# Sample attention: the K and V page loads issued by one engine, GpSimd, with the next chunk's K ahead of the chunk's V

## What is computed

```python
def _sample_attend(q, k, v, lam, rel_bias, cache_k, cache_v, page_table):
    def one(args):
        pt, qi, ki, vi = args
        kp = cache_k[pt].reshape(past, N_ATT_HEADS, 2, ATT_HEAD_DIM)
        vp = cache_v[pt].reshape(past, N_ATT_HEADS, ATT_V_DIM)
        kf = jnp.concatenate([kp, ki.astype(kp.dtype)], axis=0)
        vf = jnp.concatenate([vp, vi.astype(vp.dtype)], axis=0)
        return _diff_attention(qi[None], kf[None], vf[None], q_pos, k_pos, rel_bias, lam)[0]
    return lax.map(one, (page_table, q, k, v))
```

## Time and profile before

| | |
|---|---|
| runs, median (lowest to highest) | 3984.93 us (3982.57 to 3989.07) |
| profiled execution, its own time | 3991.51 us |
| its span, first to last instruction | 3989.5 us |
| the stage `sample_attention` in it | 649.3 to 1019.6 us |
| busy over the span: PE, DVE, ACT, POOL | 60%, 64%, 37%, 33% |
| traffic of the core's DMA engines over the span | 337 GB/s |

### The profile page before, as it was taken

How to read it: one execution, slowest core, us unless ns; L and a number is a source line. 1 busy time by engine, 2 the same in 40 slices (tenths; PEclk the granted TensorE clock), 3 DMA queues, 4 the chain that set the end, 5 groups by cost and what they waited for, 6 DMA issues and landing times. The chain is left out here.

```text
span 3989.5 us, 55293 instructions
## 1 busy us (share of the span) xinstructions
PE 2409.4 (60%) x16678; PEld 1084.2 (27%) x16678; DVE 2542.6 (64%) x6416; ACT 1465.6 (37%) x4223; POOL 1296.8 (33%) x1334
## 2 busy tenths in 40 slices
PE   5999776898765354553564465465356456446543
PEld 3446445565322121220121121122112112112110
DVE  1111165666475888677677677767757767767775
ACT  0110053333003455543434444444444344444443
POOL 0000001444002344443444344444344444444442
PEclk7999978999887565775675676566567567657655
DMA  9102134999328899999999999999999999999998
GB/s 359 49 33 61 24 1 144 407 411 387 138 92 315 353 396 404 421 420 421 411 417 413 419 415 418 403 421 412 421 407 418 419 406 420 421 420 414 419 412 333
DMA packets 245932, 1343.89 MB, mean 337 GB/s; under 512 B 47288, under 2 KB 60825, under 8 KB 94084
## 3 DMA queue, kind: packets, MB, share of 16 engines
q0 software_dynamic: 164352, 1174.49, 71.4%
q1 hardware_dynamic: 64072, 147.14, 10.9%
q10 hardware_dynamic: 17212, 18.74, 1.4%
HBM read 1319.30 MB, written 20.97 MB: 336 GB/s over the span
## 5 line engine op out<-in xcount | busy, mean ns | idle before, releaser
L1595 PE MATMUL psum<-sb_ring,sb_fold_weighted 128*32 128x256 f32 x8448 | 1008.9, 569 | 1307.6 <-PEq L62 1203.0
L1563 POOL DMA_INDIRECT sb_ring<-in_uv,sb_experts x1056 | 1151.4, 1090 | 1655.6 <-POOLq L62 1504.6
L1780 DVE CUSTOM_DVE_ANT_0 sb_ring<-sb_ring,sb_h_four 128x1024 f32<-128x1024 f32 x1056 | 1265.8, 1225 | 652.6 <-DMA sb_ring<-in_uv,sb_experts 615.4
L1595 PEld LDWEIGHTS psum<-sb_ring,sb_fold_weighted 128*32 128x32 f32 x8448 | 268.6, 134 | 2012.8 <-issue 2003.2
L1685 ACT ACTIVATE sb_gelu<-sb_dots 128x1 f32<-128x1 f32 x1056 | 210.3, 199 | 994.4 <-ACTq L62 985.8
L806 POOL DMA_DIRECT2D sb_v_pages<-in_cache_v x256 | 135.0, 527 | 861.5 <-issue 683.5
L1690 ACT ACTIVATE sb_fold_weighted<-sb_fold,sb_expert_w 128x32 f32<-128x32 f32 x1056 | 339.3, 321 | 34.4
L1618 PE MATMUL psum<-sb_w_pq,sb_h2T 128*128 128x512 f32 x576 | 336.6, 738 | 1.5 <-issue 1.5
L1687 ACT ACTIVATE sb_expert_w<-sb_gelu,sb_gates 128x1 f32<-128x1 f32 x1056 | 311.1, 295 | 34.5
L1664 ACT COPY sb_h_four<-sb_h_tiles 32x1024 f32<-32x1024 f32 x180 | 187.5, 1042 | 4.2
L1618 PEld LDWEIGHTS psum<-sb_w_pq,sb_h2T 128*128 128x128 f32 x576 | 132.4, 242 | 193.4 <-issue 193.4
(11 more groups left out here) (227 smaller groups left out, 2646.7 us busy)
## 6 DMA issues: line engine op xcount, KB each, us to landing
sb_k_pages<-in_cache_k SPq DMA_DIRECT2D x256, 256.0 KB, 6.1
sb_v_pages<-in_cache_v POOLq DMA_DIRECT2D x256, 256.0 KB, 6.2
sb_w_ada<-in_w_ada SPq DMA_DIRECT2D x12, 2048.0 KB, 17.0
sb_ring<-in_uv,sb_experts POOLq DMA_INDIRECT x1056
sb_w_qkv<-in_w_in SPq DMA_DIRECT2D x3, 2048.0 KB, 19.3
sb_w_bcu<-in_w_in SPq DMA_DIRECT2D x12, 512.0 KB, 6.3
sb_w_pq<-in_w_pq SPq DMA_DIRECT2D x3, 2048.0 KB, 17.1
sb_h_tiles<-h_scratch SPq DMA_DIRECT2D x9, 512.0 KB, 9.2
```

The lines of the kernel that those rows point to most:

```text
L1563: pool.indirect_dma_start(ring[:, slot, :], None, uv, bass.IndirectOffsetOnAxis(ap=experts[:, u, g, n:n + 1], axis=0))\
L1595: ins = nc.tensor.matmul(psum[q * NS:(q + 1) * NS, bank, at:at + QUARTER], fw[:, slot, :], ring[:, slot, D + q * QUARTER:D + (q + 1) * QUA ...
L1780: dot = nc.vector.tensor_tensor_reduce(ring[:, slot, 0:D], ring[:, slot, 0:D], h2x[:, half], 1.0, 0.0, ALU.mult, ALU.add, dots[:, slot:slo ...
```

## The change

K's loads leave SP and go to POOL. POOL first runs the K load of chunk 0; then for each k it runs the K load of chunk k+1 and then the V load of chunk k. SP keeps the small tables, which it now fetches one after another. The helper `load`, the slots, the sizes and everything the other engines do are as they were.

```diff
@@ -814,19 +814,19 @@
                 sp.dma_start(rel[0:BUCKETS, :], A["rel_bias"]).then_inc(T["small"], 16)
                 sp.dma_start(hot[:], A["const_tail"]).then_inc(T["small"], 16)
                 sp.wait_ge(T["tab"], 16)
-                cache_k = A["cache_k"][0].rearrange("g p h m d -> g p (h m d)")
-                for k in range(STEPS):
-                    load(sp, cache_k, kp, k_land, k_free, k)
-                    if k == 0:
-                        sp.wait_ge(T["rows_zero"], 1)
-                        for h in range(H):
-                            sp.dma_start(rows[head(h, M), :], A["const_rows"][h * M:(h + 1) * M, :]).then_inc(T["small"], 16)
+                sp.wait_ge(T["rows_zero"], 1)
+                for h in range(H):
+                    sp.dma_start(rows[head(h, M), :], A["const_rows"][h * M:(h + 1) * M, :]).then_inc(T["small"], 16)
 
             @block.gpsimd
             def _(pool):
                 pool.wait_ge(T["tab"], 16)
                 cache_v = A["cache_v"][0].rearrange("g p h d -> g p (h d)")
+                cache_k = A["cache_k"][0].rearrange("g p h m d -> g p (h m d)")
+                load(pool, cache_k, kp, k_land, k_free, 0)
                 for k in range(STEPS):
+                    if k + 1 < STEPS:
+                        load(pool, cache_k, kp, k_land, k_free, k + 1)
                     load(pool, cache_v, vp, v_land, v_free, k)
```

## The result

| | before | changed |
|---|---|---|
| median of the runs | 3983.75 us (4 runs) | 4251.77 us (4 runs, 4246.65 to 4255.52) |
| profiled execution: time, span | 3991.51, 3989.5 us | 4251.70, 4249.7 us |
| `sample_attention`, its first DMA to the next stage's first | 371.4 us | 636.0 us |
| from there to the end | 2968.8 us | 2969.5 us |

The ratio is 1.067, with a 95% interval of 1.0651 to 1.0688. The loss lies in the one stage: 264.6 us. The stage itself began 5.1 us sooner in this execution (644.2 instead of 649.3 us), and what follows took 0.7 us more.

What follows compares the result with a forecast made beforehand. POOL's issue stream was to bound the stage: 127 loads at 4.51 us, plus a slower first pair and breaks, 592 us, ending the stage 251 us later; adjusted to the runs' median, 4236 us, range 4214 to 4285 us.

Steps and rivals of the forecast that it cites:

- The bound: In `sample_attention`, POOL's stream issues two loads per step, 9.02 us against 5.2 us now, and becomes the slowest part.
- the two limits: In the stage before the change, TensorE busy 251.35 of 280 us and DMA traffic at 410 GB/s, both near their limit.
- The price of a load: On POOL's sequencer, 4.51 us per load: four page numbers about 2.2 us, four DMA instructions 2.26 us.
- The breaks: In POOL's stream of 128 loads: 24 short ones of 0.3 us, 7 us, and four long ones, 12 us.
- The sum: POOL's first load to its 128th: 572.8 + 0.4 + 7 + 12 = 592 us, moving the stage's end by 251 us.
- POOL finds its slots free: In POOL's queue, V loads would not wait for slots, since 7.8 us a step is under 9.26.
- the loop through V's slots: From `values` through V's and K's loads, landing and TensorE's pass: 7.8 us a step, 8.5 with a lower clock.
- The clock: TensorE, idle part of each step, begins passes at 1.2 GHz; a pass lasts some 6.3 us, still hidden.
- rival 1: TensorE stays at the lower clock all pass, 10.1 us a step, so POOL waits for V slots: 4292 us; chance 0.11.
- Rival 2: In the stage, POOL isn't the bound and K waits may be saved: 3969 to 3985 us; chance 0.03.
- point of decision: On POOL's sequencer, 2.6 us per load, two in a 5.2 us step, from which the not-slower case decides.
- Rival 3: Page numbers hidden, but one queue ties K's lead to V's slots: 6.7 us a step, 4087 us; chance 0.03.

## Why the prediction held, and where it didn't

*The bound.* Right: POOL's issue stream became the bound. Of the two limits that I had named for the kernel before, the run with K's pages in plain order points to TensorE's pass and not to the data rate. 4236 us were predicted, 4252 measured; the stage was forecast 251 us longer and was 264.6 us longer.

*The price of a load.* Right: 4.51 us in the changed kernel as in the earlier trace rows, for K and V alike. The run with added reads shows that its idle half is the reads (2.18 us for four), and the version with fixed pages that it goes with them.

*The breaks.* Four long ones, as forecast, of 4.88 to 5.18 us: 2.6 us over the plain idle time of 2.25 in three of them and 2.9 in the fourth, 10.8 us in all and not 12. The count was a guess from two, and it held. The short ones stand again at the forecast rate, every 5.3 loads.

*The sum.* 592 us forecast from the first to the last load's DMA, 603.7 measured. What failed is the step "POOL finds its slots free". By the earlier trace rows I had put the loop through V's slots at 7.8 to 8.5 us a step, under 9.26. But TensorE's pass at the end of a sample is longer, and at the lower clock the loop goes over. At 742.30 it shows: the K load issued at 726.63 reached TensorE at 733.00, 6.4 us later (I had 5.8), and POOL's V load went out 9.3 us after that (I had 6.3 for the pass and 0.5 for the step to POOL):

```profile
726.63 2.26 POOL L806 DMA_DIRECT2D sb_k_pages<-in_cache_k  x4 [2.55 <-issue]
...
733.00 3.67 PE L849 MATMUL psum<-sb_ident,sb_k_pages 128*128 128x128 f32 x16 [5.41 <-DMA sb_k_pages<-in_cache_k]
...
740.57 1.06 PE L897 MATMUL psum<-sb_v_pages,sb_probsT 128*8 128x128 f32 x32
```

The 17 loads have 51.3 us of idle time, of which 17 x 2.25 = 38 are reads; 13 us are waiting, 10 of them at the ends of the first seven samples. Four V slots took just these 13 us away, and left 590.3 us from the first to the last load's DMA, against the 592 of the sum. The tail after the last load was 1.9 us longer, too (27.9 instead of 25.9 us, from the last load to the next stage), as TensorE came to it at the lower clock (its last `values` took 1.88 us instead of 1.06). 12 + 2 us are the difference in the stage.

*The clock.* Right in kind, and true of some passes only: many passes after idle time begin at the lower level (1.2 GHz). Here, in the changed kernel, 16 transposes after 5.08 us of idle time take 3.67 us; after 2.17 us they take 3.49:

```profile
903.73 3.67 PE L849 MATMUL psum<-sb_ident,sb_k_pages 128*128 128x128 f32 x16 [5.08 <-DMA sb_k_pages<-in_cache_k]
...
907.34 1.94 PE L859 MATMUL psum<-sb_k_pagesT,sb_q_rows 128*32 128x512 f32 x8
...
913.13 3.49 PE L849 MATMUL psum<-sb_ident,sb_k_pages 128*128 128x128 f32 x16 [2.17 <-DMA sb_k_pages<-in_cache_k]
...
916.55 1.06 PE L859 MATMUL psum<-sb_k_pagesT,sb_q_rows 128*32 128x512 f32 x8
```

The score behind them is once at 1.94 us and once at 1.06: some passes are slow in part only, as I took for all, and some further on, as rival 1 had for all. And some aren't slow at all: of the 61 whole groups of transposes from 660 us on 23 took 1.94 to 1.97 us, after up to 3.15 us of idle time, and 38 took 2.7 to 3.7; of the 64 scores 40 took 1.06 or 1.07. So the forecast's picture, every pass low at its start and high at its end, was a mean between the two kinds, and near enough.

*The rivals.* Rival 2's point of decision, 2.6 us for a load, agrees with the runs with four V slots: at 2.1 us a load the version is at the old time, at 3.4 us (reading once) it isn't. Its gain didn't come. Rival 3 had the mechanism right and the size wrong. Its 6.7 us a step were made of a landing of 3.5 us after the last DMA and of a pass at the upper clock, 4.84 us. Measured with fixed pages: V's DMAs 2.1, K's first DMA to TensorE 6.3, a pass at partly lower clock 6.2, the step to POOL 0.3, 14.9 us for two steps. It is mostly the pass that was mis-sized, 6.2 instead of 4.84, and with it the way of K's pages, 6.3 instead of 5.8; the ends of samples come on top: from the first load to the last a step took 7.9 us on average (645.9 to 1149.9 us for 63.5 steps), and the time was 4147 us instead of 4087 (4083 by the 5.18 us a step of now). The forecast itself didn't hang on it, as the issue price was above it.

*The rule of the Trainium skill* (page "DMA: Bandwidth & Descriptors", section "Issuing engines are not separate DMA queues"). The changed kernel's stage is 265 us longer and, with no reads and a fourth V slot, as long as before. So the part of the rule that all issuing engines share the same DMA engines agrees with that version: one queue moved 394 GB/s where two had moved 410. Its other part, that the sequencer's issue time is small beside the transfer, is not so here: 4.51 us of issue for a chunk against 2.6 us of data at 410 GB/s.

## What to carry to other kernels

Before DMAs are moved onto one engine, add up its sequencer's stream over a step, register loads and assertions included, and set that against the step; the page's busy time doesn't have it, but the spacing of issues with free slots does. Then look for a second loop: in a queue where a load waits for a buffer, every load behind it waits too, and its lead is gone; here that alone cost 160 us, and one more buffer undid it. When two limits lie close together, removing one shows little (40 or 13 us of the stage here, where both gave 168), and only both together tell what each is worth.

## What the runs showed of the hardware

The long breaks in POOL's stream go by the count of its DMAs: 2 in 256 in the kernel before, 4 in 512 in the changed one, the first right after the 128th DMA in both, and the next 100 to 120 DMAs apart. They don't come from two engines issuing at once, and not from register addresses: the version with fixed pages and four V slots has four in 512 as well, of 2.2 to 3.3 us, the first after its 128th DMA:

```profile
738.82 2.10 POOL L808 DMA_DIRECT2D sb_v_pages<-in_cache_v  x4 [3.28 <-issue]
...
805.10 2.10 POOL L808 DMA_DIRECT2D sb_k_pages<-in_cache_k  x4 [2.17 <-issue]
```

SP had none of that length in its 512 DMAs: its longest DMA instruction took 1.72 us against a median of 0.47, and up to the last load no two loads lay more than 1.3 us further apart than the plain 4.86. What POOL waits for there is open.

A register load of a page number, with its arithmetic and assertion, costs about as much as a DMA's issue: 2.18 us for four on POOL, against 2.26 us for its four DMA instructions.
